# Constant products on TensorE at the heads of thirteen dense stages

## The reference

```python
for l in range(DEPTH):
    x = x + FFN_RES_WEIGHT * swiglu_ffn(rms_norm(x, ffn1_norm_g[l]), ffn1_w_in[l], ffn1_w_out[l])
    proj = rms_norm(x, mix_norm_g[l]) @ w_mix_in[l]
    ...
    x = x + jnp.concatenate([y_rwkv, y_moba], axis=-1) @ w_mix_out[l]
    x = x + memory_cross_attention(rms_norm(x, xattn_norm_g[l]), rms_norm(mem, mem_norm_g[l]),
                                   xattn_w_q[l], xattn_w_kv[l], xattn_w_o[l])
    x = x + FFN_RES_WEIGHT * swiglu_ffn(rms_norm(x, ffn2_norm_g[l]), ffn2_w_in[l], ffn2_w_out[l])
...
merged = jax.nn.sigmoid(g_m) * (hm @ w_br_m[l]) + jax.nn.sigmoid(g_d) * (hd @ w_br_d[l])
x = x + gate1 * (merged @ w_out[l])
x = x + gate2 * hierarchical_moe(...)
```

## Time and profile before

| what | us |
|---|---|
| median of 3 runs | 2492.67 |
| lowest and highest | 2491.08, 2494.81 |
| profiled execution | 2491.27 |
| its span, first to last instruction | 2489.5 |
| TensorE busy with matmuls | 2103.3 (84%) |
| VectorE, ScalarE, GpSimd busy | 1611.2, 1048.7, 307.3 |
| mean granted TensorE clock | 0.902 |

### The profile page before, as it was taken

How to read it: one execution, slowest core, us unless ns; L and a number is a source line. 1 busy time by engine, 2 the same in 40 slices (tenths; PEclk the granted TensorE clock), 3 DMA queues, 4 the chain that set the end, 5 groups by cost and what they waited for, 6 DMA issues and landing times. The chain is left out here.

```text
span 2489.5 us, 38512 instructions
## 1 busy us (share of the span) xinstructions
PE 2103.3 (84%) x15876; PEld 1913.8 (77%) x15876; DVE 1611.2 (65%) x2031; ACT 1048.7 (42%) x1551; POOL 307.3 (12%) x181
## 2 busy tenths in 40 slices
PE   7799797798979897979788978896983547999999
PEld 7697776697879887979588977895982447788887
DVE  6954544664696588654537558754437754799997
ACT  4232433343423433333424343234334232677775
POOL 1900003000090045000220006300000000000000
PEclk9999877899989998989698989997996577899999
DMA  9453320152455355533004236541530021699995
GB/s 366 172 202 119 143 78 2 55 184 86 185 186 196 127 226 194 186 118 136 1 3 169 102 120 235 192 179 68 186 119 1 0 91 68 240 370 370 371 369 205
DMA packets 56557, 399.69 MB, mean 161 GB/s; under 512 B 6248, under 2 KB 7424, under 8 KB 8416
## 3 DMA queue, kind: packets, MB, share of 16 engines
q1 hardware_dynamic: 52320, 370.05, 40.0%
q0 software_dynamic: 4096, 27.64, 2.9%
HBM read 396.60 MB, written 1.06 MB: 160 GB/s over the span
## 5 line engine op out<-in xcount | busy, mean ns | idle before, releaser
L310 DVE TENSOR_TENSOR weights_lo<-ring,weights_hi 128x1024 fp32r<-128x1024 f32 x696 | 920.9, 1370 | 235.0 <-ACT weights_hi L301 232.3
L324 PE MATMUL ps<-act_hi,weights_hi 128*128 128x256 f32 x2560 | 751.4, 293 | 201.0 <-DVE weights_lo L310 118.2
L301 ACT CAST weights_hi<-ring 128x1024 fp32r<-128x1024 f32 x696 | 691.1, 1046 | 359.0 <-PE ps L326 317.5
L325 PE MATMUL ps<-act_lo,weights_hi 128*128 128x256 f32 x2560 | 745.9, 291 | 0.0
L326 PE MATMUL ps<-act_hi,weights_lo 128*128 128x256 f32 x2560 | 744.9, 291 | 0.0
L324 PEld LDWEIGHTS ps<-act_hi,weights_hi 128*128 128x128 f32 x2560 | 514.7, 201 | 209.4 <-DVE weights_lo L310 177.1
L325 PEld LDWEIGHTS ps<-act_lo,weights_hi 128*128 128x128 f32 x2560 | 514.7, 201 | 1.5
L326 PEld LDWEIGHTS ps<-act_hi,weights_lo 128*128 128x128 f32 x2560 | 513.5, 201 | 0.0
L600 ACT ACTIVATE mlp_silu<-mlp_silu 128x512 f32<-128x512 f32 x44 | 27.9, 633 | 304.9 <-DVE mlp_silu L635 304.9
L324 PE MATMUL ps<-weights_hi,mlp_hidden_hi 128*128 128x512 f32 x352 | 139.3, 396 | 0.0
L325 PE MATMUL ps<-weights_lo,mlp_hidden_hi 128*128 128x512 f32 x352 | 138.8, 394 | 0.0
(11 more groups left out here) (459 smaller groups left out, 3011.3 us busy)
## 6 DMA issues: line engine op xcount, KB each, us to landing
ring<-stream SPq DMA_DIRECT2D x348, 1024.0 KB, 4.8
modulation_rows<-ada_in POOLq DMA_DIRECT2D x24, 1024.0 KB, 5.2
consts<-w_consts SPq DMA_DIRECT2D x1, 1376.0 KB, 7.9
x<-x_in SPq DMA_DIRECT2D x1, 1024.0 KB, 5.0
mem<-mem_in POOLq DMA_DIRECT2D x1, 1024.0 KB, 9.9
bias_slid<-bias_scratch SPq DMA_DIRECT2D x1, 1024.0 KB
out<-x SPq DMA_DIRECT2D x4, 256.0 KB, 2.1
lora_up<-lora_up_in POOLq DMA_DIRECT2D x1, 512.0 KB, 12.9
```

The source lines that it names most:

```text
L301: core.nc.scalar.copy(self.hi[:, i % self.ways, part], core.slot(self.start + i)[:, part]).then_inc(self.rounded.sem, 1)
L310: core.nc.vector.tensor_tensor(self.lo[:, i % self.ways, part], core.slot(self.start + i)[:, part], self.hi[:, i % self.ways, part].bitcas ...
L324: nc.tensor.matmul(out, lhs[0], rhs[0], start=start, stop=False, **kw)
L325: nc.tensor.matmul(out, lhs[0], rhs[1], start=False, stop=False, **kw)
```

## The change

A new helper issues `n` matmuls of the constant `ones` (128x128) with the first 512 columns of the constants, float32, into one PSUM bank that nobody reads. It is called in TensorE's program ahead of the first product of thirteen stages: 8 times at nine heads (two of them in `projections_stage`, two in `mix_in_stage`, five in `linear_stage`), 7 times at the three `ffn_stage` heads with `start` > 0, and 20 times instead of 8 at `w_br_m`. That is 3 x 7 + 9 x 8 + 20 = 113 matmuls. They wait for no semaphore and signal none.

```diff
+    def hold_clock(self, n, bank):
+        for _ in range(n):
+            self.nc.tensor.matmul(self.ps[:, bank, :], self.const("ones"), self.consts[:, 0:512], start=True, stop=True)
...
@@ linear_stage, TensorE
             acts.tensor(pe)
+            core.hold_clock(20 if key[0] == "w_br_m" else 8, 6)
             for c in range(n):
                 weights.await_split(pe, c)
@@ ffn_stage, TensorE
+            if start:
+                core.hold_clock(7, 0)
             gate_up(0, 0, 0, first=True)
@@ mix_in_stage, TensorE
             acts.tensor(pe)
+            core.hold_clock(8, 6)
             for c in range(n):
@@ projections_stage, TensorE
+            core.hold_clock(8, 7)
             for c in range(n):
```

## The result

| | before | changed |
|---|---|---|
| median of 10 runs | 2491.27 us | 2498.48 us |
| lowest to highest | 2486.99 to 2494.81 | 2489.04 to 2502.08 |
| profiled execution | 2491.27 | 2498.37 |
| its span | 2489.5 | 2496.6 |
| mean granted clock | 0.902 | 0.921 |

The ratio is 1.0027 with a 95% interval of 1.0016 to 1.0038: slower by 6.7 us, by little but clear of no change. (Ratios here are the ones measured over all runs of both kernels, with their intervals. They are not quotients of the two medians, and for small groups of runs the two can differ by some us.) I had forecast 2497.8, 0.2% up, with 2491.5 to 2503 as the range. TensorE's clock is higher in the mean than before and the kernel is slower all the same.

A forecast was written before the change was run, and what follows sets the result against it. TensorE, busy at a 0.50 clock at thirteen stage heads, was taken to set those stages' ends; 11.2 + 4.9 - 2.5 - 5.9 - 1.3 - 1.3 = +5.1 us on a 2492.67 median gave 2497.8 us, range 2491.5 to 2503.

The forecast's parts named there:

- What bounds the kernel and the two prices: Thirteen stage heads: TensorE busy but cold, 4.48 us each; warm start saves 1.96; a constant product costs 1.71 cold, 0.85 warm.
- When the constants can start: At the heads: the previous block's end holds TensorE at a barrier; constants start at once when the new block opens.
- `w_br_m`: Its head opens cold; twenty products make the first real one 13.2 us late, 1.96 returns: +11.2 us.
- Projections: `projections_stage`, both layers: opens cold, first real product 4.4 us late, less 1.96; +4.9 us for both.
- The ffn heads: Three `ffn` heads: seven products end 0.9 us late, less 1.96, so -1.0; second layer's `ffn1` -0.4; together -2.5 us.
- `xattn_o` and `w_out`: Three heads: products end before the first real one, 1.6 us ahead at `xattn_o`; clock stays; 3 x -1.96 = -5.9 us.
- The norm heads: Both `mix_in` layers and `w_in`: idle time after eight products; one falls cold, others keep the clock half the time; -1.3 us.
- I put nothing else down: Rest of the kernel: other engines issue nothing more and the bank written is unread, so no further term was counted.
- B: Rival, chance 0.18: all three norm heads stay warm and cold starts are short; sum +0.2, 2493 us, no change.
- Rival C: Chance 0.10: clock falls despite the holds at `xattn_o`, `w_out`, `ffn1`, losing up to 6.3 us; about +11, 2503 us.
- D: Rival, chance 0.05: a constant product costs one pass, not four; no head late, some 6 us gained, 2487 us.
- E: Rival, chance 0.05: TensorE passes on before other engines finish, so holds start behind its last real work; -19, 2474 us.

The follow-up runs named there:

- fitted kernel: Changed kernel with float32 constant products per head fitted to the time available (w_br_m 3, projections 3, ffn 6, others 7 to 12): 2459.51 us, ratio 0.9880.
- the one with 452 short products: Changed kernel with 16-bit one-pass constant products, four times as many at each head: 2492.26 us, ratio 1.0006; again 2492.43, 1.0010.

## Why the prediction was right, step by step

**What bounds the kernel and the two prices.** Right. Real products at 0.120 and 0.213 us, a constant one at 0.85 and 1.71: eight took 7.1 us at `xattn_o` (6.83), 9.3 at the cold projections (9.07), and the twenty were over 18.4 us after the block's start at `w_br_m` (19.3; its clock rose after 2.9 us and not 4.5). In the second profile of the changed kernel the clock rose there after 4.9 us, and the first real product came 19.3 us after the opening.

**When the constants can start.** Right, and the step that decided the sign. The constants start 0.03 us after ScalarE's first operation in every block whose first work on TensorE they are.

**The heads.** `w_br_m` +10.8 for +11.2, by two misses that nearly cancel: the first product was 12.2 us late and not 13.2, and 1.4 came back and not 1.96. Projections +5.8 for +4.9: the products lasted 9.3 us and not 9.1, and the saving was 1.5 to 2 us. A small term was missing here. Where the constants run straight into the real products, the second of these follows after 0.52 us, behind a wait after 0.19, so a late head gives some 0.3 us less than I counted. The ffn heads -2.9 for -2.5: the clock did not fall in the gap behind the transposes at `ffn1`, so the -0.4 there should have been -1.0. `xattn_o` and `w_out` -6.3 for -5.9. `w_br_d` -0.9 for -1.3. The norm heads -1.1 for -1.3, but in the wrong places, and that the sum is near is luck: `mix_in` of the second layer was counted at about -1 and gave -0.1, `w_in` was counted at -0.3 and gave -1.0. Sum +5.5 for +5.1.

**"I put nothing else down".** This step was wrong in the single stage and nearly right in the sum. Stretches that the change leaves alone moved by up to 4 us (`ffn1`) and balanced to +1.6. My range had room for that as "the runs' own scatter". A part of it is more than scatter: in pairs of profiles it repeats for a kernel. In the fitted kernel's profile it was worth 10.8 us, the main reason why my 18 to 19 us there fell short of 30.

**The total.** The time forecast, 2497.8, lies 0.7 us from the one measured, the difference forecast, +5.1, lies 1.6 from the +6.7 of the ratio. The closer agreement of the times is luck: I counted from a median of three runs that was 1.4 us above that of ten. That the result is clear of no change was no strong forecast either, for I gave slower 0.48 and same 0.42. What the runs bear out is the mechanism and most of the terms. Rival C's sum has a small slip: 2492.67, 5.1 and 6.3 make 2504, not 2503.

**The rivals.** B did not come (`mix_in` fell cold again in both layers), nor C (`xattn_o` stayed warm with 1.3 us left). D was true of a kernel that I had to build for it. E was excluded by the 10.48 us for which TensorE stood in front of the barrier.

## What to carry to other kernels

A wait has to be measured from where an engine may enter it, and not from where the engine last worked. 16.6 us of idle time before the first product of `w_br_m` were 10.5 us behind a barrier and 6.2 in which filler could run, and filler sized for the first number cost 11 us. Filler that waits for nothing must end before the operands are ready at the granted clock that it will have: three cold products did all that was wanted where twenty stood. If it ends some 6 us too early, it brings next to nothing. When a change moves waits of a few microseconds about, price the clock at all later waits as unknown: against the one profile of before, the stretches without an edit made between 4 us more and 11 us less here, and compare kernels by stages before believing a sum.

## What the runs showed of the hardware that I had not expected

The clock rose early enough behind three float32 constants of 128x512 started cold (4.54 us in all, the clock full from 3.45 us behind the start) that none of the 96 real products of `w_br_m` ran cold. Whether the clock falls in a wait of 2.5 us is not a matter of its length alone: behind 2.45 us in `w_in` of the changed kernel the real products were warm, behind 2.54 in `mix_in` cold for 2.9 us. Some such outcomes repeat in two profiles of the same kernel: `ffn1` of the second layer was 2.8 and 4.4 us longer than before in two profiles of the changed kernel, 0.5 and 0.6 shorter in two of the one with 452 short products. Others do not, and the times of one kernel follow them: among executions of the kernel before, a mean clock higher by 0.005 went with a time shorter by some 6 us.
